# Row scales turned by TensorE, and another order of the last layer's projections in a fused three-layer kernel

## The reference, cut to what matters

```python
x = first_block(...)                      # two layers, ends with rms_norm(x, final_norm_g)
h = rms_norm_2(x, norm_g)                 # per token: x * rsqrt(mean(x*x) + eps) * gain
(q, kc, vc, ks, vs, kw, vw, gl, g_nsa, rwkv_in, g_rwkv) = _split(h @ w_in, IN_SIZES)
# compress_blocks, for kc and vc: blocks of 32 tokens, stride 16, 31 of them
blk = concatenate([ch[:, :, :-1], ch[:, :, 1:]], axis=3) + pos_emb
k_cmp = silu(blk.reshape(B, G, -1, 32 * 64) @ w1) @ w2        # w1: 2048 x 256
g = sigmoid(gl)                           # 24 branch gates for each token
o = g0 * o_cmp + g1 * o_sel + g2 * o_win  # three attention branches
return x + mix @ w_out                    # mix: gated NSA and RWKV outputs
```

## Time and profile before

| what | value |
| --- | --- |
| median of three runs | 1227.66 us (1226.94 to 1229.54) |
| the profiled execution's own time | 1229.92 us |
| its span, first to last instruction | 1228.1 us |
| PE busy | 1140.7 us, 93% |
| DVE busy | 603.1 us, 49% |
| ACT busy | 513.5 us, 42% |
| POOL busy | 435.2 us, 35% |
| mean granted TensorE clock | 0.984 of full speed |

### The profile page before, as it was taken

The page is one execution under the profiler, slowest core; times in us unless marked ns, Lnnn a source line. Parts: engine busy times, 40 slices in busy tenths (PEclk is TensorE's granted clock), DMA queues, the critical chain, the costliest instruction groups (busy, mean ns, idle before and its releaser), DMA issues.

```text
span 1228.1 us, 24858 instructions
## 1 busy us (share of the span) xinstructions
PE 1140.7 (93%) x10339; PEld 956.0 (78%) x10339; DVE 603.1 (49%) x1379; ACT 513.5 (42%) x1039; POOL 435.2 (35%) x375
## 2 busy tenths in 40 slices
PE   3999999999898999899998994988999999999995
PEld 3988887889898998665798994966777787678862
DVE  5000002841728257788417344027884897335547
ACT  4232224952424432688623353342884431233321
POOL 5744484884445435301345334330006341000000
PEclk9999999999999999999999997999999999999999
DMA  7433243323121222200231225262002232100001
GB/s 212 143 104 97 77 135 103 81 61 104 45 94 48 91 94 78 69 1 1 70 103 36 70 69 128 73 185 69 2 1 70 69 94 92 55 23 3 4 2 69
DMA packets 74394, 89.87 MB, mean 73 GB/s; under 512 B 3073, under 2 KB 67722, under 8 KB 74154
## 3 DMA queue, kind: packets, MB, share of 16 engines
q1 hardware_dynamic: 70136, 78.65, 20.4%
q0 software_dynamic: 2416, 8.26, 2.7%
q10 hardware_dynamic: 1730, 1.38, 0.6%
HBM read 84.01 MB, written 4.26 MB: 72 GB/s over the span
## 4 chain that ended last, share of the span: by engine, by line
PE 75%; DVE 11%; ACT 6%; issue 3%; POOL 2%; DMA 2%; ACTq 1%; DVEq 0%; POOLq 0%
PE bank L477 70%; PE bank L769 2%; ACT arena L1330 2%; POOL ring_parts L2607 1%; DVE stat L1856 1%; DVE stat L1857 1%; DVE arena L1875 1%; ACT ring_parts L1359 1%; PE bank L679 1%; PE bank L953 1%; DVE arena L1867 1%; ACT arena L1446 1%; DMA token_scales<-stat 1%; ACT arena L1709 1%; ACT arena L1339 1%
## 5 line engine op out<-in xcount | busy, mean ns | idle before, releaser
L2607 POOL TENSOR_TENSOR ring_parts<-ring,ring_parts 128x512 fp32r<-128x512 f32 (+1 forms) x236 | 310.6, 1349 | 421.7 <-ACT ring_parts L1359 330.2
L477 PE MATMUL bank<-ring_parts,hT_parts 128*128 128x256 f32 x1536 | 310.1, 285 | 8.4 <-ACT hT_parts L1364 3.6
L477 PE MATMUL bank<-ring_parts,arena_parts 128*128 128x256 f32 x1344 | 291.9, 286 | 21.1 <-POOL ring_parts L2607 16.4
L477 PEld LDWEIGHTS bank<-ring_parts,hT_parts 128*128 128x128 f32 x1536 | 247.6, 192 | 10.4 <-POOL ring_parts L2607 3.7
L477 PEld LDWEIGHTS bank<-ring_parts,arena_parts 128*128 128x128 f32 x1344 | 225.4, 192 | 23.3 <-POOL ring_parts L2607 16.7
L477 PE MATMUL bank<-hT_parts,ring_parts 128*128 128x512 f32 x692 | 231.2, 394 | 0.0
L477 PE MATMUL bank<-arena_parts,ring_parts 128*128 128x512 f32 x652 | 226.4, 399 | 2.8 <-POOL ring_parts L2607 2.8
L1330 ACT ACTIVATE arena<-bank 128x512 f32<-128x512 f32 (+5 forms) x295 | 139.9, 541 | 188.8 <-PE bank L477 184.9
L477 PE MATMUL bank<-arena 64*64 64x64 f32 (+7 forms) x2288 | 176.8, 300 | 7.7 <-ACT arena L1709 2.9
L477 PEld LDWEIGHTS bank<-arena 128*64 128x64 f32 (+3 forms) x2288 | 119.2, 144 | 52.8 <-issue 18.9
L477 PEld LDWEIGHTS bank<-hT_parts,ring_parts 128*128 128x128 f32 x692 | 130.6, 189 | 30.7
(11 more groups left out here) (259 smaller groups left out, 1425.1 us busy)
## 6 DMA issues: line engine op xcount, KB each, us to landing
ring<-in_a_w_in SPq DMA_DIRECT2D x16, 1024.0 KB, 5.4
ring<-in_w_in SPq DMA_DIRECT2D x15, 1024.0 KB, 5.5
ring<-in_b_w_in SPq DMA_DIRECT2D x10, 1024.0 KB, 5.1
ring<-in_ple_w_gate SPq DMA_DIRECT2D x8, 1024.0 KB, 5.2
arena<-rpb_rows POOLq DMA_DIRECT2D x16, 256.0 KB, 3.5
ring<-in_a_w_out SPq DMA_DIRECT2D x4, 1024.0 KB, 5.1
ring<-in_b_w_out SPq DMA_DIRECT2D x4, 1024.0 KB, 5.0
ring<-in_w_out SPq DMA_DIRECT2D x4, 1024.0 KB, 5.1
```

Source lines behind the costliest of these rows:

```text
L477: return nc.tensor.matmul(o, l, r, start=start, stop=stop)
L2607: nc.gpsimd.tensor_tensor(rounded(r), r, read_back(high_slot(n)[:, o:o + m // 4]), ALU.subtract)\
```

## The change

There are four parts. The scales no longer go through DRAM: DVE spreads them on a diagonal (`diag`, 128x512), and PE multiplies it with ones after the third tile of `Csel`, eight small products for `scol` and two of 512 columns for `srow`; DVE copies both out, putting the row in natural order. DVE copies the two banks of `Ckv` to SBUF (`kv_raw`) before it makes the reciprocal roots, and lays out `fl` from there. The order of the halves becomes `Ckv`, `Csel`, `("Cq", 0)`, `Cwin`, `("Cq", 1)`, `("W1K", 0)`, `("W1V", 0)`, `Cbg`, `("W1K", 1)`, `("W1V", 1)`, and PE makes the first part of `hid` before the branch gates and the second part behind them; `bgT` moves into the transposes of q and k. On ACT the high part of `("Cq", 0)` is made ahead of the wait for `fin_rstd`, that of `("Cog", 0)` ahead of the tanh of the branch gates. DVE makes the rotary embedding before it takes the branch gates.

```diff
@@ -213,12 +212,12 @@
-        for name, a, b in (("Ckv", 512, 768), ("Csel", 768, 1024), (("Cq", 0), 0, 256), (("Cq", 1), 256, 512),
-                           ("Cwin", 1024, 1280), ("Cbg", 1280, 1408)):
+        for name, a, b, n in (("Ckv", 512, 768, None), ("Csel", 768, 1024, None), (("Cq", 0), 0, 256, None),
+                              ("Cwin", 1024, 1280, None), (("Cq", 1), 256, 512, 0), ("Cbg", 1280, 1408, 1)):
             load(name, cols(w_in2, a, b), (KB, b - a))
-        for n in range(2):
-            for name, w in (("W1K", A["cmp_w1_k_2"][0]), ("W1V", A["cmp_w1_v_2"][0])):
-                load((name, n), w[1024 * n:1024 * n + 1024].rearrange("(k p) n -> p k n", p=P), (8, 256), False)
+            if n is not None:
+                for kv, w in (("W1K", A["cmp_w1_k_2"][0]), ("W1V", A["cmp_w1_v_2"][0])):
+                    load((kv, n), w[1024 * n:1024 * n + 1024].rearrange("(k p) n -> p k n", p=P), (8, 256), False)
         for n in range(2):
@@ -344,6 +341,8 @@
         gains2 = stat[:, 184:192]
+        kv_raw = area(18624, 1024).rearrange("p (n t) -> p n t", n=2)
+        diag = area(20480, T)
         o_high = area(0, 4096)
@@ -824,43 +823,63 @@
-            def tokens(name, key):
+            def tokens(name, key, behind=None):
                 need3(name)
...
                     tm3((key, i), "a", W3(name), i, 0, act2)
+                    if behind:
+                        behind(i)
                 used3(name)
-            tokens("Csel", "sel")
+            def token_scales(i):
+                if i != 2:
+                    return
+                pe.wait_ge(S("scale_diag"), 1)
+                b = begin("scol", "v")
+                for m in range(NT):
+                    for e in range(2):
+                        ins = mm(b[64 * e:64 * e + 64, m:m + 1], ap(diag, [(GR, GW)], 2 * m + e), C("ones64")[:, 0:1],
+                                 True, True)
+                end(ins)
+                b = begin("srow", "v")
+                for e in range(2):
+                    ins = mm(b[64 * e:64 * e + 64, :], C("ones64"), diag, True, True)
+                end(ins)
+            tokens("Csel", "sel", token_scales)
             tokens(("Cq", 0), "q0")
+            tokens("Cwin", "win")
             tokens(("Cq", 1), "q1")
-            tokens("Cwin", "win")
+            def hidden(n):
+                for ii in range(8 * n, 8 * n + 8):
+                    for m, name in enumerate(("W1K", "W1V")):
+                        if ii % 8 == 0:
+                            need((name, n))
+                        ins = mm(hid_bank[64 * m:64 * m + 64, 0:256], fl[:, m, ii * 64:ii * 64 + 64],
+                                 W((name, n))[:, ii % 8, :], ii == 0, ii == 15)
+                return ins
+            pe.wait_ge(S("C_flat"), 2)
+            hid_bank = begin("hid", "v", apart=True)
+            hidden(0)
             need3("Cbg")
...
-            pe.wait_ge(S("C_flat"), 2)
-            b = begin("hid", "v", apart=True)
-            for ii in range(16):
-                for n, name in enumerate(("W1K", "W1V")):
-                    if ii % 8 == 0:
-                        need((name, ii // 8))
-                    ins = mm(b[64 * n:64 * n + 64, 0:256], fl[:, n, ii * 64:ii * 64 + 64], W((name, ii // 8))[:, ii % 8, :],
-                             ii == 0, ii == 15)
-                if ii == 7:
-                    pe.wait_ge(S("bg_tanh"), 1)
-                    bt = begin("bgT", "a")
-                    for i in range(NT):
-                        turned_gates = nc.tensor.transpose(bt[:, i * 24:i * 24 + 24], thC[0:24, 0, i * P:(i + 1) * P],
-                                                           ident[0:24, 0:24])
-                    end(turned_gates)
-                    used3(("W1K", 0))
-                    used3(("W1V", 0))
-            end(ins, "hid")
+            used3(("W1K", 0))
+            used3(("W1V", 0))
+            end(hidden(1), "hid")
             used3(("W1K", 1))
...
             for i in range(NT):
+                if i == 1:
+                    pe.wait_ge(S("bg_tanh"), 1)
+                    bt = begin("bgT", "a")
+                    for m in range(NT):
+                        turned_gates = nc.tensor.transpose(bt[:, m * 24:m * 24 + 24], thC[0:24, 0, m * P:(m + 1) * P],
+                                                           ident[0:24, 0:24])
+                    end(turned_gates)
                 for name, src in (("qp", q2), ("qr", q2r)):
@@ -1599,9 +1618,8 @@
                 square("norm2", i, 20)
+            high(HI[("Cq", 0)])
             act.wait_ge(S("fin_rstd"), 1)
-            act.dma_start(bass.AP(scale_rows.tensor, 0, [[1, CT], [GW, GR], [CT, NT]]), stat[:, 36:40],
-                          allow_slow_non_contiguous=True).then_inc(s_rows, 16)
@@ -1609,12 +1627,7 @@
             x_final(1)
-            act.wait_ge(s_rows, 16)
-            act.dma_start(srow, bass.AP(scale_rows.tensor, 0, [[0, P], [1, T]])).then_inc(s_scale, 16)
-            act.dma_start(scol, bass.AP(scale_rows.tensor, 0, [[1, P], [P, NT]]),
-                          allow_slow_non_contiguous=True).then_inc(s_scale, 16)
             x_final(2)
-            x_final(3)
@@ -1630,12 +1643,12 @@
-            act.wait_ge(s_scale, 32)
-            high(HI[("Cq", 0)])
+            x_final(3)
+            evacuated(act, "srow")
             keys_values(0, "sel")
             for n in range(2):
-                high(HI[("Cq", n)] + 1)
+                high(HI["Cwin" if n == 0 else "Cbg"])
                 for l in range(2):
@@ -1643,18 +1656,19 @@
                     give(copy(q2r[:, i, 256 * n:256 * n + 256], b[:, 0:256], scol[:, i:i + 1]), key)
-            high(HI["Cbg"])
-            keys_values(1, "win")
+                if n == 0:
+                    high(HI[("Cq", 1)])
+                    keys_values(1, "win")
+            high(HI[("Cog", 0)])
             evacuated(act, "bg")
             nc.scalar.activation(thC[0:24, 0, :], thC[0:24, 0, :], ACT.Tanh, scale=0.5).then_inc(S("bg_tanh"), 1)
-            b = take(act, "bgT")
-            give(copy(gt[:, :, :], b[:, 0:96].rearrange("p (i n) -> p i n", i=NT)), "bgT")
             b = take(act, "hid")
...
             for i in range(NT):
-                if i == 2:
-                    high(HI[("Cog", 0)])
+                if i == 1:
+                    b = take(act, "bgT")
+                    give(copy(gt[:, :, :], b[:, 0:96].rearrange("p (i n) -> p i n", i=NT)), "bgT")
                 for name, dst in (("qp", qTp), ("qr", qTr)):
@@ -2146,6 +2160,10 @@
                     times_gain(i)
+                for n in range(2):
+                    key = ("kvc", n)
+                    b = take(dve, key)
+                    give(nc.vector.tensor_copy(kv_raw[:, n, :], b[:, :]), key)
                 dve.wait_ge(S("ss_norm2"), NT)
@@ -2153,6 +2171,8 @@
                 dve.sem_inc(S("fin_rstd"), 1)
+                TT(diag.rearrange("p (i q) -> p i q", i=NT), ap(ident, [(0, NT), (1, P)]),
+                   ap(stat[:, 36:40], [(1, NT), (0, P)]), ALU.mult).then_inc(S("scale_diag"), 1)
@@ -2163,13 +2183,15 @@
             dve.wait_ge(S("low_home"), 1)
-            take(dve, ("kvc", 0))
             nc.vector.memset(fl[:, :, :], 0.0).then_inc(S("C_flz"), 1)
             dve.wait_ge(S("C_flz"), 1)
-            dve.wait_ge(s_scale, 32)
+            b = take(dve, "scol")
+            give(nc.vector.tensor_copy(scol, b[:, 0:NT]), "scol")
+            b = take(dve, "srow")
+            give(nc.vector.tensor_copy(srow.rearrange("p (r c) -> p r c", r=GR), ap(b[:, :], [(1, GR), (GR, GW)])), "srow")
+            evacuated(dve, "srow")
             for n in range(2):
-                key = ("kvc", n)
-                b = take(dve, key)
+                b = kv_raw[:, n, :]
                 m = 0
@@ -2179,12 +2201,8 @@
                             ins = TT(dst, src, s, ALU.mult)
-                            m += 1
-                            if m < 8:
-                                ins.then_inc(S("C_flcopy"), 1)
-                give(ins, key)
-                dve.wait_ge(S("C_flcopy"), 7 * (n + 1))
-                evacuated(dve, key)
+                            ins.then_inc(S("C_flcopy"), 1)
+                dve.wait_ge(S("C_flcopy"), 8 * (n + 1))
                 pos = vcol("posk" if n == 0 else "posv", 0, 16)
@@ -2197,9 +2215,7 @@
-            b = take(dve, "bg")
-            give(TT(thC[0:24, 0, :], b[0:24, :], srow[0:24, :], ALU.mult), "bg")
-            evacuated(dve, ("win", NT - 1))
+            evacuated(dve, ("q1", NT - 1))
             for n, (src, dst) in enumerate(((q2, q2r), (kd, kd))):
@@ -2218,11 +2234,13 @@
                 dve.wait_ge(S("C_rope"), 2 * n + 2)
-            evacuated(dve, "bgT")
-            link(TS(gt[:, :, :], gt[:, :, :], 0.5, 0.5, ALU.mult, ALU.add))
+            b = take(dve, "bg")
+            give(TT(thC[0:24, 0, :], b[0:24, :], srow[0:24, :], ALU.mult), "bg")
             b = take(dve, "hid")
...
```

(9 more changed lines are left out.)

## The result

| kernel | median, us | ratio to the kernel before, 95% interval |
| --- | --- | --- |
| before | 1228.18 | |
| changed | 1218.74 (1217.86 to 1220.69) | 0.9926 [0.9914, 0.9939] |

The change is faster by 9.4 us of median, and the interval of the ratio leaves out 1. I forecast 16.1 less, 1211.5 us, with 1217.0 as the upper end of the range: the sign was right, the size was not. (The prediction counts from 1227.66, the median of three runs; a fourth run is in the 1228.18.)

What follows compares the result with a forecast made beforehand. PE, 75% of the chain, bounds the kernel. Removing 16.45 idle and 2.3 clock, adding 1.2, with the reorder paying 4.5 and 2.1 and returning 2.84, 1.6 and 0.7, gives 16.1 us less: 1211.5 us, range 1208.5 to 1217.

Steps and rivals of the forecast that it cites:

- the early high part: ACT makes `("Cq", 0)`'s high part at 735.3 to 737.2, POOL ends by 743.1, covered by at least 1.4 us.
- a gain under 11 us: Sign for the whole kernel: such a gain would mean a wait counted as covered is not.
- The scale products: On PE after three of `Csel`'s four tiles: cost 0.5 to 1.9 us, taken as 1.2.
- the DRAM round trip: Before `("Cq", 0)`: PE's idle 16.45 us and 2.3 us of clock go.
- the three halves without a stop: After `Csel`, PE runs three halves of 11.3 us each without waiting, from 744.5 to 778.4.
- the new stop: Before `hid`'s second part, PE waits 5.3 us for the load of `("W1V", 1)`, from 787.8 to 793.1.
- `hid`'s slow second part: After the stop for `("W1V", 1)`, half clock adds 0 to 2.5 us to 3.7; 2.1 taken.
- A: POOL and DVE block each other more, at `Cwin`'s low part: two waits per piece stall 2.2 us; 1214 to 1215.5; chance 0.10.
- B: ACT's stand in `high(("Cog", 0))` becomes the bound before `gate_c(0)`: 2.2 us more, 1213.7 us; chance 0.11.
- C: Clock stays at half through the transposes into `gate_c(0)`: 1.6 us more on `hid`, 1.5 on gates, 1214.6; chance 0.10.
- D: ACT's wait for x to be written out stalls PE at `("Cq", 1)`: 7.8 us, 1219.3, or slower than before; chance 0.02.
- E: The stall is smaller or PE's clock doesn't fall in it, and the scales cost 0.5 us: 1209 us; chance 0.05.

Runs made afterwards that it cites:

- e1: Changed kernel with POOL waiting for DVE's diagonal of scales before the low part of `("Cq", 0)`: 1213.22 us, 0.9900 of the kernel before.
- e2: Changed kernel with `("W1V", 1)` and `("Cog", 0)` allowed to load once `hid`'s first part is done: 1209.31 us, 0.9864 of the kernel before.
- e9: Kernel before, scales still through DRAM, with only the new order of halves, projections, `hid`, `bgT` and gates: 1231.17 us, ratio 1.0025.
- e7: Changed kernel with POOL's low part of `("Cq", 0)` cut into 16 pieces instead of 4: 1213.87 us, 0.9895 of the kernel before.

## Why the prediction was wrong

**The step that failed** is that of the early high part: "now the high part follows at once [...] under DVE's reciprocal roots", with POOL's pieces behind it. I checked what POOL's result was needed for, and not whom POOL would run beside. In the kernel before, the roots had no POOL beside them: they ended at 738.18, and POOL began at 753.96. The rule of the Trainium skill that I cited, "SBUF — State Buffer", "Who interferes with whom", said it, and the addition in the earlier trace rows showed it; I applied both to `Cwin`'s low part, where DVE's layout had over 20 us of slack, and dismissed `("Cq", 0)` as beside "only one large operation". Small operations suffer most: each of 0.17 us waited for a piece of 1.25. The wait that I put at nothing is thus DVE's, 4.0 us on roots and diagonal against a cover of 1.4 to 1.7. No rival priced it. Price: the stop, 2.3 us, and the clock behind it, 0.9 on the products (2.87 less 1.97) and 1.6 up to `hid` (38.6 from 743.20 to 781.77, against 37.0 in e1). The clock's share is of one execution: in e2, behind the same stop, it was 1.4 instead of 2.5. The prediction had a sign for this: a gain under 11 us means "that a wait I have counted as covered is not".

**A term that was mis-sized.** The scale products: 1.2 us taken, 2.0 measured (e1), 0.8 more and just above the upper end of 0.5 to 1.9. The main cause is a misreading of rows: the x32 and x30 of `hid` are records, two for each plain float32 product, so my description's 64 matmuls of `hid` are 32 products, of 0.23 us each. The two products of 512 columns are four records and took 0.99 us in e1, not the 0.46 of my lower end; the eight small ones took 0.98, where I had 0 to 0.9. With that, the sum of the stretch is closed: 2.3 + 0.8 + 2.5 = 5.6 of the 6.2 us missing; 0.3 more lie between the products and `hid` and 0.2 behind it.

**What held.** The reasoning for the DRAM round trip (16.45 and the clock behind it go), the three halves without a stop (47.5 us from `Csel` to `hid` in e1, 46.4 forecast plus 0.8), the new stop (5.3 forecast, 4.86), `hid`'s slow second part (5.8 forecast, 6.03), the start of `gate_c(0)` behind it (6.1 forecast, 5.9 measured), its price (5.7). `hid`'s start to the second layer: 32.3 forecast, 32.5 measured. That the new order costs cover is confirmed by e9, its remedy by e2.

**The rivals.** A had the blocking of POOL and DVE, but at the wrong place and with the wrong engine waiting: it priced what POOL loses at `Cwin`. There POOL ended at 756.7 and PE did not wait, though DVE's eight products beside it took 8.68 us, against 4.3 to 4.4 for such eight before. B did not come: ACT's high part ended at 801.5, before `hid` at 802.7. C did not: PEclk was 1.00 from 802.66. D did not: x was written out in time (3.0 us from issue to landing, the median of four), and PE had no stop at `("Cq", 1)`. E did not: the stop was 4.86 us and the clock fell.

The range failed for the same reason as the forecast: it held A to C, one at a time or two in part, and no stall at the scales with its clock.

## What to carry to other kernels

When work is moved ahead to fill a wait, list what runs on the other engines in its new place, and in particular whether POOL then works beside a chain of small DVE operations with two SBUF inputs; make POOL wait for that chain (e1), or cut its pieces (e7). When a ring frees its slots by the last finished result, ask at what point each load may start in the new order; a finer signal (e2) turned a loss of 3 us into a gain of 1.4 to 5. Price a product from a row only after counting how many records one such product has.

## What the runs showed of the hardware that I had not expected

DVE's products for `fl` had one input in a bank before and have both in SBUF now. In the changed kernel eight of them took 8.68 us beside POOL's four pieces (749.64 and 750.57, above). DVE's timeline of the kernel before, where POOL worked from 753.96 to 759.90:

```profile
752.03 4.29 DVE L2181 TENSOR_TENSOR arena<-bank,cst 64x248 f32<-64x248 f32 x8 [11.50 <-issue]
...
758.80 4.37 DVE L2181 TENSOR_TENSOR arena<-bank,cst 64x248 f32<-64x248 f32 x8
```

There eight took 4.3 to 4.4, though POOL worked beside the greater part of the first eight. That the inputs in SBUF alone don't make the products slow is seen in the changed kernel, where POOL stood idle beside the first eight:

```profile
744.04 4.43 DVE L2203 TENSOR_TENSOR arena<-arena,cst 64x248 f32<-64x248 f32 x8
```

POOL's pieces took 6.17 us, and 5.04 without DVE's work beside them. So of the waiting 4.25 us fell on DVE, the engine with the small operations, and 1.1 on POOL.

After a stop of 2.3 us PE ran at 1.2 GHz (PEclk 0.50 from 740.33); after one of 2.85 it did so for a part of `gate_c(0)` in one execution of a kernel (PEclk 0.64) and not in the other, a difference of 2.8 us on one product. Differences of this size between single profiled executions are therefore no evidence on an edit.
